# Two ends of the prompt-mixer stage: gate sigmoids and key transposes moved into the input stage, the output norm's weight multiplied into z beforehand, and its closing barrier without the GpSimd drain

## The reference

```python
def hybrid_layer(x, ...):
    u = rmsnorm(x, g_mix)
    proj = einsum('btd,df->btf', u, w_in)      # q, kv, g_nsa, qkv_gdn, b, a, z, q_mem, g_br
    o_nsa = nsa_core(q, ..., g_nsa)            # sparse attention, three branches, merged by sigmoid(g_nsa)
    o_gdn = gdn_mixer(qkv_gdn, b, a, z, ...)   # gated DeltaNet
    o_mem = mem_attend(qm, mem_kv)
    ...                                        # branch products, gates, w_out, MLP

def nsa_core(...):
    kcmp = compress_blocks(cmp_kv[:, :, 0], ...)     # keys and values in blocks of 32 tokens, through a small MLP
    ...
    g = sigmoid(gates)
    o = g[..., 0:1] * o_cmp + g[..., 1:2] * o_sel + g[..., 2:3] * o_win

def gdn_mixer(...):
    ...
    o, s_new = gated_delta_chunked(q, k, v, g, beta, s0)
    o = rmsnorm(o, o_norm) * silu(z)           # rmsnorm(x, g) = x * rsqrt(mean(x*x) + eps) * g
```

## Time and profile before

| | us |
|---|---|
| median of 3 runs | 1552.63 |
| lowest, highest | 1546.97, 1557.31 |
| the profiled execution, its own time | 1557.42 |
| its span in the trace | 1555.6 |

### The profile page before, as it was taken

The page is one execution under the profiler, slowest core; times in us unless marked ns, Lnnn a source line. Parts: engine busy times, 40 slices in busy tenths (PEclk is TensorE's granted clock), DMA queues, the critical chain, the costliest instruction groups (busy, mean ns, idle before and its releaser), DMA issues. The chain is left out here.

```text
span 1555.6 us, 27068 instructions
## 1 busy us (share of the span) xinstructions
PE 1430.7 (92%) x11344; PEld 1317.2 (85%) x11344; DVE 857.2 (55%) x1559; ACT 399.0 (26%) x912; POOL 80.5 (5%) x74
## 2 busy tenths in 40 slices
PE   6999999999888897979668799999999999999998
PEld 5888899899877786868445698999999999999998
DVE  3465266877464565555434536545558556365563
ACT  3544023322351443444233410001121001010000
POOL 1000001100011111111000000000000000000000
PEclk8999999999978896979889799999999999999999
DMA  9133025222342000010656523322341322323221
GB/s 363 64 136 109 28 86 194 82 82 86 99 163 109 1 1 0 2 54 1 224 223 217 196 69 109 109 89 88 111 148 55 109 82 87 104 81 107 83 82 56
DMA packets 115648, 159.03 MB, mean 102 GB/s; under 512 B 6039, under 2 KB 106839, under 8 KB 112778
## 3 DMA queue, kind: packets, MB, share of 16 engines
q1 hardware_dynamic: 111886, 122.76, 24.3%
q0 software_dynamic: 2304, 33.56, 5.5%
q10 hardware_dynamic: 1348, 1.12, 0.2%
HBM read 145.04 MB, written 16.66 MB: 104 GB/s over the span
## 5 line engine op out<-in xcount | busy, mean ns | idle before, releaser
L330 PE MATMUL ps<-hH,wh 128*128 128x260 f32 x512 | 145.0, 283 | 0.9 <-DVE hT L301 0.9
L330 PE MATMUL ps<-mergedH,wh 128*128 128x260 f32 x512 | 145.7, 285 | 0.0
L330 PE MATMUL ps<-mergedT,wh 128*128 128x260 f32 x512 | 144.9, 283 | 0.0
L330 PE MATMUL ps<-hT,wh 128*128 128x260 f32 x512 | 144.8, 283 | 0.0
L330 PE MATMUL ps<-mergedH,wl 128*128 128x260 f32 x512 | 144.5, 282 | 0.0
L330 PE MATMUL ps<-hH,wl 128*128 128x260 f32 x512 | 144.5, 282 | 0.0
L330 PE MATMUL ps<-uH,wh 128*128 128x260 f32 x480 | 138.2, 288 | 0.0
L462 PE MATMUL ps<-XT,w 128*128 128x256 f32 (+1 forms) x512 | 124.2, 385 | 0.3 <-DVE hbias L615 0.3
L330 PE MATMUL ps<-uL,wh 128*128 128x260 f32 x384 | 109.5, 285 | 0.0
L330 PE MATMUL ps<-uH,tw 128*128 128x260 f32 x384 | 109.4, 285 | 0.0
L462 PEld LDWEIGHTS ps<-XT,w 128*128 128x128 f32 x512 | 93.0, 192 | 11.3 <-issue 0.9
(11 more groups left out here) (565 smaller groups left out, 3554.9 us busy)
## 6 DMA issues: line engine op xcount, KB each, us to landing
wt<-in_w_ff SPq DMA_DIRECT2D x32, 1024.0 KB, 5.3
wt<-in_w_in SPq DMA_DIRECT2D x15, 1024.0 KB, 5.3
tw<-in_w_in SPq DMA_DIRECT2D x12, 1024.0 KB, 5.2
ring<-in_cache_mem_kv SPq DMA_DIRECT2D x4, 2048.0 KB, 8.3
w<-in_cmp_w SPq DMA_DIRECT2D x8, 512.0 KB, 7.7
ring<-in_cache_win_kv SPq DMA_DIRECT2D x2, 2048.0 KB, 8.8
out_s_win<-in_cache_win_kv SPq DMA_DIRECT2D x1, 4088.0 KB
scratch_uhigh<-uH SPq DMA_DIRECT2D x1, 2080.0 KB
```

What stands on the lines that cost most here:

```text
L330: ins = pe.matmul(out, lhsT(i, c), rhs(j, c), start=(first and c == 0 and k == 0), stop=(last and c == chunks - 1 and k == 2))
```

## The change

1. **Gate sigmoids.** The five sigmoids go from the start of the mixers to the input stage, behind the sigmoid of beta. `gate` is allocated there.
2. **Key transposes.** The eight transposes become the last work of PE in the input stage (`cmp_turn`), into banks 2 and 3, each once that bank's last unit has been copied out. In the mixers DVE copies one bank to `XT` and ACT the other (`keep_turned`), each first in its queue. The scores no longer wait for these copies; the first transposition into bank 2 and the first product into bank 3 do.
3. **z.** silu is applied tile by tile behind the copy of each unit of the last weight tile. DVE multiplies each prompt tile by `gdn_o_norm`. The samples' tile is not multiplied.
4. **Tile end.** DVE scales the state before it sums the squares. The three products (inverse root, weight, silu(z)) become four `scalar_tensor_tensor` instructions of DVE, one for each head, that read `o` in PSUM and write z. POOL's two products go, and ACT's next squares wait for DVE's sum instead.
5. **Small moves.** The copy into `qmpad` (ACT) and the copy of `cTs` (DVE) go a little back in the mixers.
6. **End of the mixers.** The block closes with `no_gpsimd_drain=True`, `retire()` is skipped behind it (its semaphores are cleared one stage later), and SP does not wait for the stored state. That wait goes to DVE before it writes the second output buffer of the samples' stage, which may lie where the state lay, and to SP at the end of the tail.

```diff
@@ build
             for s in stages:
                 s()
+                if s == self.stage_prompt_mixers:
+                    continue
                 self.retire()
@@ stage_inputs, DVE
+                for k, u in enumerate(z_units[0:TT]):
+                    yield at[u + 1] + 1.2
+                    z = heads(z_of(P, units[u][2]))
+                    dve.wait_ge(z_silu, k + 1)
+                    ch.step(dve.tensor_tensor(z, z, self.V("gdn_o_norm").unsqueeze(1).broadcast_to([P, GH, GD]), ALU.mult))
@@ stage_inputs, PE
+                def cmp_turn():
+                    yield at[NU] + 1.0
+                    pe.wait_ge(chain, ready["k", TT])
+                    for q in range(2):
+                        u = max(u for u in range(NU) if u % 4 == 2 + q)
+                        pe.wait_ge(kept[0 if by_act[u] else 1], count[u])
+                        for c in range(4):
+                            a = C_KV + c % 2 * P
+                            ins = pe.transpose(ps[:, 2 + q, c * P:(c + 1) * P], proj[:, 2 * q + c // 2, a:a + P], ident)
+                        ins.then_inc(self.cmp_turned, 1)
@@ stage_inputs, ACT
+                    for t in range(TT + 1):
+                        act.activation(self.gate[0:rows(t), t, :], proj[0:rows(t), t, C_GN:C_GN + 24], ACT.Sigmoid)
...
-                    evicted(act, NU - 1)
-                    act.activation(z(P, slice(0, TT)), z(P, slice(0, TT)), ACT.Silu)
-                    act.activation(z(NB, TT), z(NB, TT), ACT.Silu)
+                    for u in z_units:
...
+                        yield at[u + 1] + 0.4
+                        evicted(act, u)
+                        act.activation(z_of(rows(t), t), z_of(rows(t), t), ACT.Silu).then_inc(z_silu, 1)
@@ delta_act
-        g2.wait(act, "gated", t - 1)
+        v.wait(act, "so", t - 1)
@@ delta_dve
         yield key(t, 12)
+        if t:
+            p.wait(dve, "o", t)
+            ch.step(dve.tensor_tensor(state[:, :, :], state[:, :, :], bc(sc[:, EL, :]), ALU.mult))
...
-            ch.step(dve.tensor_tensor(state[:, :, :], state[:, :, :], bc(sc[:, EL, :]), ALU.mult))
...
-        v.done(dve.tensor_tensor(sq[:, 0:GH, :], bank(0), bc(so), ALU.mult), "out", t)
+        for h in range(GH):
+            ins = dve.scalar_tensor_tensor(z[:, h, :], ps[:, 4, h * P:(h + 1) * P], so[:, h:h + 1], z[:, h, :], ALU.mult, ALU.mult)
...
-        if t == TT - 1:
-            ch.step(dve.tensor_tensor(sq[:, 0:GH, :], sq[:, 0:GH, :], heads(self.V("gdn_o_norm")), ALU.mult))
-            ch.step(dve.tensor_tensor(z, z, sq[:, 0:GH, :], ALU.mult))
@@ delta_pool
-        if t == TT - 1:
-            return
-        g2.done(pool.tensor_tensor(sq[:, 0:GH, :], sq[:, 0:GH, :], heads(self.V("gdn_o_norm")), ALU.mult), "normed", t)
-        g2.done(pool.tensor_tensor(z, z, sq[:, 0:GH, :], ALU.mult), "gated", t)
@@ stage_prompt_mixers
-        with nc.Block() as block:
+        with nc.Block(no_gpsimd_drain=True) as block:
@@ keep_turned: ACT for q = 1, DVE for q = 0, both at the start of their queues
+            def keep_turned(copy, q):
+                for g in range(NG):
+                    bank = ps[g * HD:(g + 1) * HD, 2 + q, :].rearrange("p (c v t e) -> p c v t e", c=2, v=2, e=2)
+                    for e in range(2):
...
+                        ins = copy(dst.rearrange("p v (c t) -> p c v t", c=2), bank[:, :, :, :, e])
@@ pair_pe
+                    if u == 0:
+                        pe.wait_ge(kept, 2)
...
-                    else:
-                        pe.wait_ge(kept, 4)
@@ stage_prompt_mixers, SP
-                sp.wait_ge(stored, 32)
@@ stage_sample_attention, DVE, and stage_tail, SP
+                if n == 1:
+                    dve.wait_ge(self.p_stored, 32)
...
+                sp.wait_ge(self.p_stored, 32)
```

More of the change, by code:

```diff
@@ L817, in stage_inputs @@
         us_ready, s_pairs, s_whole = (S("in_s_" + x) for x in ("tokens", "pairs", "whole"))
-        buf_in, convd, gates, gact, f_chain = (S("f_" + x) for x in ("buf", "conv", "gates", "gact", "chain"))
+        buf_in, convd, gates, gact, f_chain, z_silu = (S("f_" + x) for x in ("buf", "conv", "gates", "gact", "chain", "zsilu"))
+        z_units = [u for u in range(NU) if units[u][0] == NT_ - 1]
+        z_of = lambda R, t: proj[0:R, t, tok_col(C_Z):tok_col(C_Z) + GH * GD]
         groups = ("mem", "q", "m", "k")
@@ L1295, in delta_setup @@
         act_names = ["ed", "E", "sqq", "sqk", "rt", "qnT", "qeT", "knT", "kbT"] + [f"Y{l}" for l in range(1, L)] + ["nWT", "vn", "sqo", "ro"]
-        pool_names = ["e2"] + [f"Am{l}" for l in range(1, L)] + ["normed", "gated"]
+        pool_names = ["e2"] + [f"Am{l}" for l in range(1, L)]
         self.d = b
@@ L1555, in stage_prompt_mixers @@
         w_loaded = S("d_w")
[L1556 to L1557 removed]
+        kept, gelu, small_ready, small_kept = (S("d_" + x) for x in ("kept", "gelu", "small", "smallkept"))
+        gates, zeroed, stored = S("d_gates"), S("d_zeroed"), self.sem("state_stored")
+        self.p_stored = stored
         hid_kept, hid_turned, hid = S("d_hidkept"), S("d_hidturned"), Pb[0][:, 0, 0:P]
@@ L1693, in values @@
                         pe.wait_ge(o_done, u)
+                    else:
+                        pe.wait_ge(kept, 4)
                     for a in range(2):
@@ L1722, in _ @@
                 by_key(cmp_pe(pe), pair_pe(pe), *(self.delta_pe(pe, t) for t in range(TT)))
+            def keep_turned(copy, q):
+                for g in range(NG):
+                    bank = ps[g * HD:(g + 1) * HD, 2 + q, :].rearrange("p (c v t e) -> p c v t e", c=2, v=2, e=2)
+                    for e in range(2):
+                        dst = XT.rearrange("p (v g) t -> p v g t", v=2)[e * HD:(e + 1) * HD, :, g, q * P:(q + 1) * P]
+                        ins = copy(dst.rearrange("p v (c t) -> p c v t", c=2), bank[:, :, :, :, e])
+                    ins.then_inc(kept, 1)
             def cmp_act(act):
-                yield 0
-                for t in range(TT + 1):
-                    act.activation(self.gate[0:rows(t), t, :], proj[0:rows(t), t, C_GN:C_GN + 24], ACT.Sigmoid).then_inc(gates, 1)
+                yield -1.0
+                act.wait_ge(self.cmp_turned, 2)
+                keep_turned(act.copy, 1)
+                yield 4.7
                 act.wait_ge(zeroed, 3)
@@ L1782, in cmp_dve @@
             def cmp_dve(dve, ch):
-                yield 4
-                for q in range(2):
-                    dve.wait_ge(turned, q + 1)
-                    for g in range(NG):
-                        bank = ps[g * HD:(g + 1) * HD, q, :].rearrange("p (c v t e) -> p c v t e", c=2, v=2, e=2)
-                        for e in range(2):
-                            dst = XT.rearrange("p (v g) t -> p v g t", v=2)[e * HD:(e + 1) * HD, :, g, q * P:(q + 1) * P]
-                            ins = dve.tensor_copy(dst.rearrange("p v (c t) -> p c v t", c=2), bank[:, :, :, :, e])
-                        ins.then_inc(kept, 1)
+                yield -1.0
+                dve.wait_ge(self.cmp_turned, 1)
+                keep_turned(dve.tensor_copy, 0)
                 yield 33.0
@@ L1872, in _, with samples_dve @@
                 c_ch, u_ch, g_ch = Chain(d_chain, dve), Chain(v_chain, dve), Chain(self.d_chain, dve)
-                dve.tensor_copy(self.cTs[:, :, :], self.cT[:, :, SEQ:NT])
-                by_key(cmp_dve(dve, c_ch), pair_dve(dve, u_ch), *(self.delta_dve(dve, g_ch, t) for t in range(TT)))
+                def samples_dve():
+                    yield 6.0
+                    dve.tensor_copy(self.cTs[:, :, :], self.cT[:, :, SEQ:NT])
+                by_key(cmp_dve(dve, c_ch), pair_dve(dve, u_ch), samples_dve(), *(self.delta_dve(dve, g_ch, t) for t in range(TT)))
             def gather_pool(pool):
```

37 lines of the change are left out of this document (16 added, 21 removed).

## The result

| | before | after |
|---|---|---|
| median of 17 runs each, us | 1552.93 | 1540.84 |
| lowest, highest | 1542.0, 1558.81 | 1536.85, 1548.38 |
| span of the profiled execution | 1555.6 | 1538.8 |

The ratio is 0.9918, 95% interval 0.990 to 0.9935: 12 us, 0.8%. The forecast was 1540.4. The two spans differ by 16.8 us, more than the medians: the profiled execution of before took 1557.42, 4.5 us over its median, that of the changed kernel 1540.91, its median. Stage lengths are therefore read only where several profiles agree.

What follows compares the result with a forecast made beforehand. The prediction took the mixers to be bound by a chain from engine to engine, with PE waiting inside it. Its terms summed to 13.2 us, less 1 for propagation: 12.2 off 1552.6 gives 1540.4 us, range 1532 to 1547.

Steps and rivals of the forecast that it cites:

- input stage's end: Input stage: silus hidden between copies, PE last at 423.9 instead of ACT at 425.37; 1.4 us gained.
- mixers' start with its clock: Start of the mixers: first products and sum of squares earlier, 3.8 us; PE keeping full clock there, 0.9 us.
- ends of tiles 0 to 2: Mixers: four products replace one, state scaling hidden, GpSimd's collision with L1847 gone in tile 2; 1.5 us gained.
- DVE's end of tile 3: End of the mixers: state scaling leaves and DVE's last products shorten, ending at 751.03 instead of 752.77; 1.7 us gained.
- barrier: Between mixers and samples' stage: 0.5 us instead of 4.76 from DVE's end to the first product; 4.2 us gained.
- samples' stage: Samples' stage: 0.2 us lost waiting for slot 3's gather and 0.1 on later clears, 0.3 in all.
- propagation: Whole kernel: 1 us taken off for chains in which the shifted part was not the last to arrive.
- What is late next: Samples' stage: the gather lands near 755.7, PE wants slot 3 at 755.8; 0.2 us lost, SP's window load costs nothing.
- The clock giving more: Rival, mixers: shorter PE pauses also raise the granted clock, for a gain of 16 to 20 us; chance 0.20.
- The samples' stage giving it back: Rival: slot 3 or SP's loads come late and take back the barrier's 4.2, gain 7 to 9 us; chance 0.12.
- The end still waiting: Rival, mixers' end: some engine still waits for the gather, leaving a gain of about 9 us; chance 0.05.
- Slower: Rival, mixers: shifted work lowers the mean clock from 0.85; 0.76 would give 1569 us, 1% slower; chance 0.03.

Runs made afterwards that it cites:

- warm end: The changed kernel with the clearing also skipped behind the input and samples' stages, and twenty unread transposes behind PE's last mixers product: 1541.7 us, ratio 0.9929.
- filler: The kernel before with eight transposes of the identity, which nobody reads, at the input stage's end: 1553.4 us, ratio 1.0002.

## Why the prediction was right, point by point

| term | predicted, us | measured, us | from |
|---|---|---|---|
| input stage's end | 1.4 | 1.6 | last dense product to first product, 4.19 to 2.62 |
| mixers' start with its clock | 3.8 + 0.9 | 4.6 | start, 21.5 to 15.3, less the line above |
| ends of tiles 0 to 2 | 1.5 | 1.2 | tiles 0, 1, 2: 0, 0.14, 1.06 |
| DVE's end of tile 3 | 1.7 | 1.7 | from PE's end, 4.35 to 2.69 |
| barrier | 4.2 | 4.1 | 4.76 to 0.67 |
| samples' stage | -0.3 | -0.5, the rest not resolved | pause at its end, 2.6 to 3.1; its length 112.7, 110.9, 109.8 before; 109.1, 109.5 |
| propagation | -1 | -0.7 | tile 2: 1.06 gained, 0.1 to 0.4 left at tile 3 |

- *Input stage's end.* Right, PE last at 423.96 (423.9 forecast).
- *Mixers' start.* Right in size and in its parts: the sum of squares starts 5.1 us into the stage. The forecast said 5.8, but that figure left out the clock's share, which its own sum had as 0.9.
- *Clock at the start.* Right that the clock is kept, and the condition mattered more than the text said: 1.02 us of pause keep it, 2.05 and 2.65 do not. The size, 0.9, was not measured by itself; the 4.6 of the table holds both terms.
- *Tile ends.* Tile 0 costs nothing (DVE's wait for PE fell from 0.71 to 0.30, as the four products took its place). Four products of 128 take 1.13 us (1.12 forecast). In tile 1 I counted 0.28 and got 0.14: DVE's scaling now ends after ACT's square (571.79 against 571.60 in the second profile), so it isn't hidden whole. In tile 2 the collision is gone, 1.06 of 1.24. Most of this was lost again before tile 3. From tile 2's sum to tile 3's it is 85.1 to 85.2 us before and 84.8 to 85.0 after. By stretch, in the changed kernel:

```profile
661.00:665.00 4.00, 4.00 (x20) 4.00 (x21) 2.16 (x6) 1.93 (x5) 0.00 (x0) 0.50 0.00 0
665.00:667.00 2.00, 2.00 (x12) 2.00 (x11) 0.29 (x3) 0.00 (x0) 0.00 (x0) 0.50 0.00 0
667.00:669.00 2.00, 2.00 (x12) 1.07 (x10) 1.15 (x5) 1.03 (x3) 0.12 (x1) 0.88 0.00 0
```

  PE is at half clock here until 667.5 (0.88 in the last row), and before the change from 667.1 (0.89 in the stretch to 668) to 673.9. The work moved up by 7.4 us, the half clock by 6.4, so 1.0 us more of it is spent at half clock: 0.5 us back. The rest I did not trace. Nor is "no 1 us L1847", a sign that the forecast named, true of the whole stage: it holds at the tile's end only. In the second quarter of the mixers two such products, of 0.45 to 0.81 and of 1.22 or 1.23 us, stand in every profile of before and of the changed kernel, and one of 1.00 us is new in the first profile of the changed kernel (one of 1.01 stands in the second of before). GpSimd and DVE there, in order of time:

```profile
588.16 1.26 POOL L1538 TENSOR_TENSOR g_E<-g_E,consts 128x512 f32<-128x512 f32 x1 [27.17 <-ACT g_E L1419]
588.43 1.00 DVE L1869 TENSOR_TENSOR rg<-rg,gate 128x2 f32<-128x2 f32 x1
```

- *The mixers' end.* Both terms right. What the text had wrong is the way they hang together: it priced DVE's 1.7 and the barrier's 4.2 as if each stood alone. Without edit 6 DVE's part is worth nothing (pause 9.20).
- *What is late next.* Right to some tenths. PE's last product of the mixers came 6.7 us sooner than before, and the gather that is issued behind PE's work moved with it (746.97 to 740.29). Beyond that shift SP's window load moved up by 2.1 us (757.47 to 748.72; "under 2" was forecast), and slot 3 lands just as PE wants it (748.72 and 748.75), without a wait.
- *The later clears.* Forecast as 0.1, and mis-sized: PE's pause at the end of the samples' stage grew from 2.6 us in all three profiles of before to 3.1 in both of the changed kernel, and is 2.6 again with the clearing put back. So of the 0.9 us that the skipped clearing saves, 0.5 comes back one stage later.
- *The mixers' clock.* The forecast named a clock that is not within 0.02 of 0.85 as a sign of being wrong, and this sign is there: 0.88 in both profiles of the changed kernel, 0.85 in all three of before. That is 22 to 25 us less at half clock, of which 16 to 19 lie in the two pauses and the work behind them; the other 7 are in the middle of the mixers, where executions differ by more. The sum had priced the clock at the start alone.
- *Clock at the samples' start.* The sum had no term for it, though the earlier trace rows showed the clock at 0.54 in the pause. In the changed kernel the first products run at full clock, 0.64 against 1.07 us, and the half clock comes 1 us later. Its worth can't be told from chance: the stage took 109.1 and 109.5 us, and 109.8 in the third profile of before.
- *Rivals.* The clock giving more: the clock rose, but the gain of 12 us is not the 16 to 20 of that rival. The samples' stage giving it back: not by slot 3, as forecast; the later gathers do hold back what is gained ahead of them, as the warm end showed, but in the changed kernel the shift passed. The end still waiting: no, shown by its rows. Slower: no.

The terms as measured add up to 12.0 us; the medians differ by 12.1, and the ratio's interval is 10 to 15.5. That the two meet so closely, and the forecast of 12.2 with them, is in part luck. Two of the three groups of edits cost more time when taken out than their waits account for (8.6 against 5.8, and 5.6 against 2.8 us; the errors of some 3 us leave open whether that is real). Between single profiles the way from the last dense product to tile 3's sum alone shortened by 6.6 to 12.5 us, where the terms give 6.7. The waits at both ends of the stage are shown one by one; that nothing else contributed is not.

## What to carry to other kernels

A barrier waits for the slowest of several things at once. Here GpSimd's drain behind an outstanding gather and a store that SP waited for ended within 0.6 us of each other, with a clearing behind them, and an engine made faster ahead of them shortened nothing until they were gone: change such things together, or find which comes last, before you judge one alone. Work that GpSimd does "for free" beside DVE has a price where the two overlap, here 0.96 us on an instruction of 0.16, and a shift in time can bring about such an overlap elsewhere. Read a stage's length from several profiles, with the granted clock beside it, before you call a difference of 2 us a gain.

## What I had not expected of the hardware

- Two executions of the same kernel differ by up to 20 us (1539.6 and 1559.3 of span), and most of it goes with the mean granted clock (0.965 and 0.947).
- A pause of 2.65 us with eight dummy transposes ahead of it brought PE back at 1.2 GHz (filler), while after one of 3.37 us, behind dense work of tile 3, it came back at 2.4 GHz and fell 1 us later. The length of a pause alone doesn't tell what comes after it.
- GpSimd's drain lasts as long as the gather that it issued last is under way: 8.99, 9.15 and 9.37 us in three kernels, with 8.6, 8.7 and 8.9 us from the gather's issue to its landing, and none of the other engines could leave the block in that time.
